# The turn of the next block's rows, placed ahead of the down products of the last block

## What is computed

```
def moe(h, router_w, router_bias, w_gate, w_up, w_down):
    ...
    _, e_idx = lax.top_k(jnp.where(in_grp, sel, -jnp.inf), TOP_K)
    ...
    hid = jax.nn.silu(jnp.einsum('bsd,edf->bsef', h, w_gate)) * jnp.einsum('bsd,edf->bsef', h, w_up)
    return jnp.einsum('bsef,bse,efd->bsd', hid, combine.astype(h.dtype), w_down)
```

## Time and profile before

| | |
|---|---|
| median of 3 runs | 2784.15 us (2782.47 to 2786.63) |
| the profiled execution, its own time | 2785.84 us |
| its span, first to last instruction | 2784.1 us |
| TensorE busy | 2451.3 us, 88% |
| VectorE, ScalarE, GpSimd busy | 38%, 26%, 17% |
| mean granted TensorE clock | 0.927 |
| the two expert stages | about 1084 to 1384 us and 2455 to 2755 us |

### The profile page before, as it was taken

The page is one execution under the profiler, slowest core; times in us unless marked ns, Lnnn a source line. Parts: engine busy times, 40 slices in busy tenths (PEclk is TensorE's granted clock), DMA queues, the critical chain, the costliest instruction groups (busy, mean ns, idle before and its releaser), DMA issues.

```text
span 2784.1 us, 28347 instructions
## 1 busy us (share of the span) xinstructions
PE 2451.3 (88%) x10206; PEld 1638.4 (59%) x10206; DVE 1049.4 (38%) x2147; ACT 710.9 (26%) x1531; POOL 480.4 (17%) x465
## 2 busy tenths in 40 slices
PE   4999997989998887999869999979899977879996
PEld 2585675674453365776536756757645533567774
DVE  6317743334434433111163276343444254211113
ACT  2213322432341222111122232233333302311111
POOL 1003323020002230113100133220200023111240
PEclk7999998989999997999969999989999988979997
DMA  7221223132215534872162222131231345448502
GB/s 223 62 82 52 65 95 96 37 95 68 69 39 190 187 136 155 307 270 69 34 220 81 67 69 84 53 110 47 75 87 53 106 152 180 193 172 304 188 7 91
DMA packets 203433, 325.05 MB, mean 117 GB/s; under 512 B 32032, under 2 KB 165024, under 8 KB 187552
## 3 DMA queue, kind: packets, MB, share of 16 engines
q1 hardware_dynamic: 180656, 301.13, 32.0%
q0 software_dynamic: 19296, 19.98, 2.3%
q10 hardware_dynamic: 3344, 2.12, 0.2%
HBM read 348.28 MB, written 47.19 MB: 142 GB/s over the span
## 4 chain that ended last, share of the span: by engine, by line
PE 82%; DVE 7%; DMA 4%; issue 3%; ACT 2%; POOL 1%; SPq 1%; ACTq 0%; POOLq 0%; DVEq 0%
PE ps L674 76%; PE ps L672 5%; SPq L500 1%; DMA ring<-in_w_branch 1%; DVE spare L1664 1%; DVE ssq L1774 1%; DVE SC L1664 1%; DMA M<-h_rows,find_i 1%; DVE X L2143 1%; DMA Y<-y_rows 0%; DMA ring<-in_w_in 0%; DMA ring<-in_ada_w 0%; DMA bias_row<-in_router_bias 0%; POOL TM_rounded L2297 0%; ACT Y L1396 0%
## 5 line engine op out<-in xcount | busy, mean ns | idle before, releaser
L674 PE MATMUL ps<-H,ring 128*128 128x512 f32 x1280 | 610.6, 612 | 5.1 <-ACT H L1373 4.2
L674 PE MATMUL ps<-ring,H 128*128 128x256 f32 (+1 forms) x1920 | 418.4, 381 | 15.4 <-DMA ring<-in_w_in 15.4
L674 PEld LDWEIGHTS ps<-ring,H 128*128 128x128 f32 x1920 | 366.6, 195 | 66.4 <-DMA ring<-in_w_in 16.3
L674 PEld LDWEIGHTS ps<-H,ring 128*128 128x128 f32 x1280 | 232.1, 192 | 261.3 <-issue 243.3
L674 PE MATMUL ps<-Y,ring 128*128 128x512 f32 x512 | 230.8, 612 | 51.9 <-DMA ring<-in_w_branch 50.0
L674 PEld LDWEIGHTS ps<-Y,ring 128*128 128x128 f32 x512 | 100.0, 197 | 178.3 <-issue 124.9
L2438 POOL TENSOR_TENSOR Y<-M,Y 128x512 f32<-128x512 f32 x56 | 80.9, 1451 | 539.1 <-ACT Y L1534 522.8
L2257 DVE TENSOR_TENSOR SC<-SC,ps 128x256 f32<-128x256 f32 x46 | 19.4, 422 | 359.9 <-ACT SC L1611 359.9
L674 PE MATMUL ps<-Y,M 128*128 128x256 f32 x576 | 134.7, 392 | 14.1 <-ACT M L1603 11.8
L2456 POOL TENSOR_TENSOR M<-M,SC 128x512 f32<-128x512 f32 x48 | 62.9, 1312 | 433.4 <-DVE SC L2078 433.4
L1664 DVE SCALAR_TENSOR_TENSOR spare<-ring,cact,spare 128x256 f32<-128x256 f32 x280 | 137.2, 557 | 0.0
(11 more groups left out here) (343 smaller groups left out, 3411.7 us busy)
## 6 DMA issues: line engine op xcount, KB each, us to landing
ring<-in_w_in SPq DMA_DIRECT2D x272, 256.0 KB, 4.2
ring<-in_ada_w SPq DMA_DIRECT2D x192, 256.0 KB, 4.6
ring<-in_w_branch SPq DMA_DIRECT2D x64, 256.0 KB, 5.1
Y<-in_moe_w_gate SPq DMA_DIRECT2D x16, 1024.0 KB, 5.5
ring<-in_moe_w_up SPq DMA_DIRECT2D x16, 1024.0 KB, 4.9
gate_logits<-CM SPq DMA_DIRECT2D x44, 256.0 KB, 2.4
DVt<-gate_logits SPq DMA_DIRECT2D x8, 1024.0 KB, 8.0
SQKV<-gate_logits SPq DMA_DIRECT2D x8, 1024.0 KB, 7.9
```

The lines of the kernel that those rows point to most:

```text
L674: ins = nc.tensor.matmul(o, lhsT, rhs, start=start, stop=stop)
```

## The change

In all three streams (TensorE, ScalarE, VectorE) the turn of the next block's rows, with its copies, changes places with the down products of the block before, with their copies. GpSimd's and SyncE's streams stay as they are.

```
                     if j < BLOCKS:
                         gate_up(j)
+                    if j + 1 < BLOCKS:
+                        rows_turn(j + 1)
                     if j:
                         down(j - 1)
-                    if j + 1 < BLOCKS:
-                        rows_turn(j + 1)
                     if j < BLOCKS:
                         hidden_turn(j)
...
                         act(gated[i], ps[:, 4 + i, 0:FF], ACT.Silu).then_inc(silu_ready, p.gives(silu_ready))
+                    if j + 1 < BLOCKS:
+                        turn_copy(j + 1)
                     if j:
                         k = (j - 1) % 2
                         eng.wait_ge(down_done[0], p.next(down_done[0]))
                         if j >= 3:
                             eng.wait_ge(y_stored[k], p.next(y_stored[k], 16))
                         act(y_rows[k][:, 0:512], bank(6), ACT.Copy).then_inc(y_ready[0], p.gives(y_ready[0]))
-                    if j + 1 < BLOCKS:
-                        turn_copy(j + 1)
...
                             hidden_ready[i], p.gives(hidden_ready[i]))
+                    if j + 1 < BLOCKS:
+                        turn_copy(j + 1)
                     if j:
                         k = (j - 1) % 2
                         eng.wait_ge(down_done[1], p.next(down_done[1]))
                         if j >= 3:
                             eng.wait_ge(y_stored[k], p.next(y_stored[k], 16))
                         v.tensor_copy(y_rows[k][:, 512:1024], bank(1)).then_inc(y_ready[1], p.gives(y_ready[1]))
-                    if j + 1 < BLOCKS:
-                        turn_copy(j + 1)
```

## The result

The changed kernel takes 2927.44 us in the median of 4 runs (2918.05 to 2935.87), against 2785.23 us for the kernel before (2782.47 to 2786.63, 4 runs): a ratio of 1.0518, 95% interval 1.0498 to 1.0537, 142 us slower. The forecast was 2827 us with a range of 2798 to 2900. The direction and the ring were right; the time lies beyond the range, near rival A's 2913.

A forecast was written before the change was run, and what follows sets the result against it. PE's work and waits were taken to bound the kernel, afterwards the gather in plain turns. Plain turns 11, extra-expert turns 11 + 11 - 5 and clock 14 gave +42 us on 2784.15: 2827 us, range 2798 to 2900.

The forecast's parts named there:

- the ring: Expert loop: gather issue, landing, turn of the rows and down products set a 12.79 us turn; +11.0 us for 22 turns.
- rival A: Gate weights' load gets ahead of the gather on the DMA engines: 64 us plus 22 of low clock, about 2913; chance 0.22.
- The gap that closes: PE's 1.00 us between turned rows and next gate product shrinks to 0.22: 0.78 us a turn, 33 us over 42.
- D: The moment in a loop turn when PE starts what follows the down products; the gather is issued at D + 3.08.
- the clock: Longer PE waits for gathers lower the granted clock: 12 falls of 1.16 us, 14 us; none to all 36 give 0 to 42.
- The turns with extra experts: Gathers behind extra weight loads come late: +11 us for ten turns, +11 for four others, -4.7 for turns keeping their gain.

The follow-up runs named there:

- e2: The changed kernel with GpSimd issuing each gather a whole block earlier: 2743.79 us, ratio 0.9846 to the kernel before.
- e3: The kernel before, old order kept, with each gather issued a block earlier and nothing else: 2779.9 us, ratio 0.999.
- e4: The changed kernel with four unused products ahead of the turn of the rows in turns 2 to 11: 2892.55 us, ratio 1.038.
- e1: The changed kernel with the gate weights' slot given back only after the gather has landed, so their load starts later: 2850.68 us, ratio 1.0234.
- e6: The changed kernel with gathers a block earlier from block 14 on only, for the turns with extra experts: 2879.37 us, ratio 1.0347.

## Why the prediction was wrong in size

- **The gap that closes:** right. 42 x 0.78 = 33 us were forecast; e2 is 38.6 us faster than the kernel before, and by e3 some 36 of them belong to the new order.
- **The ring:** right in place and form. The gather is issued at D + 3.08, and the turn of its rows waits for it. With 9.0 us to landing the formula 3.08 + landing + 4.31 gives 16.4 us, and e4, without the low clock, has 16.44.
- **The step that failed** is the landing time put into it: "I take the median, since the down load and the scatter keep their distances to D". They did, and the down load still lands in 4.8 us. But the load of the gate weights does not keep its distance: it follows the start of the gate products, which moved from D + 1.87 to D + 0.22. It had come 3.0 us after the gather's issue and now came 1.3 us after it, while the rows were being read. The gather takes 9.0 instead of 5.4 us (8.5 in the second layer), so a plain turn waits 4.7 us in the mean (47.4 over 10) instead of 1.28. e1 and the lone gather of 1302 us show it from both sides. Over the twenty plain turns with such a gather (8.9 us in the mean in the first layer, 8.3 in the second) that is 64 us. With the 42 forecast and 27 more of low clock than were allowed for (see the clock below) it makes 133 of the 142.
- **Rival A** named exactly this and got a chance of 0.22. The prediction had no row for or against the two transfers meeting and leaned on the load coming too late, where the arithmetic (issue at D + 4.4, gather landing at D + 8.5) already had 4 us in which both were open. Its price was near, 64 us for the transfer (64 measured) and 22 for the clock (27 measured), but in part by luck: the 2.9 us a turn stood for one transfer going ahead of the other, which is not what happened, and low clock cost a turn more than the 1.16 us put in. Nor did the load go ahead of the gather as a whole, as the prediction read the rule of the Trainium skill ("DMA: Bandwidth & Descriptors", Queues, rings and completion order) that an engine drains a whole packet of one queue before it turns to the next. By this trace both queues have packets in the same stretch, both DMAs get longer, by 3.8 and 3.2 us against the earlier trace rows, and both land together (1237.6 and 1238.0 in the turn above). Where a single engine changed queues the rows do not show.
- **The clock:** 14 us were allowed, 12 falls at 1.16. It fell in 18 of the 20 plain turns with a gate load behind the gather, and a plain turn lost about 2 us by it (e4), 41 us of busy time in all. Of the ten waits forecast at 1.9 us, counted as half, eight came at that length and did not lower it (the other two were of 2.21 and 3.04 us, and it fell): after the 1.85 us above, the turn of the rows and the down products ran in 0.99 and 3.44 us. And the fall hits another part than assumed: the turned rows and the down products that follow the wait, which lie on the ring, and not gate and up, where it would be hidden.
- **The turns with extra experts:** nearly right. Forecast were +22 us, less 3 for the turns that close a gap and plus 10 for nine of the twelve clock falls, 29 in all. e6 takes back 48 us, of which 18 x 0.78 = 14 are gaps closed beyond the kernel before; the 34 left stand against the 29.

## What to carry to other kernels

Before a step is moved earlier, work out how much slack each of its inputs keeps, from the event that issues the input and not from the place where it used to be needed: here 9.2 us became 4.1 for a DMA that took 5.4. Then list which other transfers are issued from events that the same edit moves, since a transfer's duration from the old trace holds only with the old neighbours. The cure was cheap: with the gather issued one block earlier the same reordering turns from 5.2% slower to 1.5% faster than the kernel before.

## What the runs showed of the hardware

- A gather of rows of 4 KB (0.30 MB for the one alone in the earlier trace rows) and a 1 MB weight load on another queue slow each other when the load is issued 1.3 us after the gather. Against the same two 3.0 us apart, the gather goes from 5.4 to 9.0 us (medians of the plain turns of the first layer) and the load from 5.0 to 8.2 (the turns shown).
- After the waits of 3.6 to 5.8 us in ten plain turns of the changed kernel the granted clock of the next 7 us was 0.57 to 0.81, 0.69 in the mean, so part of them at 1.2 GHz, and the turn of the rows and the down products took 5.7 to 7.3 us. After the wait of 1.85 us they took 4.4, at a clock of 1.00. Between these the length of the wait alone did not decide: after one of 2.21 us the clock fell, after one of 3.32 us it did not, and in e4 it fell after one of 1.88 us.
- Products that fill the wait bring the clock back to 0.99, and in this kernel wasted work on PE saved 35 us.
